# A fused mask-and-maximum pass in the second block's softmax, with the query sums put into the masks by GpSimd

## The reference

```python
def forgetting_attention(q, k, v, f, qnorm_g, knorm_g, f_bias):
    ...
    logf = jax.nn.log_sigmoid(f.astype(F32) + f_bias.astype(F32))
    c = jnp.cumsum(logf, axis=1).transpose(0, 2, 1)
    ...
        s = s + c[:, :, lo:hi, None] - c[:, :, None, :hi]
        s = jnp.where(k_pos <= q_pos, s, -jnp.inf)
        p = jax.nn.softmax(s, axis=-1).astype(dt)
```

## Time and profile before

| what | value |
|---|---|
| median of 3 runs | 1545.66 us (1545.61 to 1547.28) |
| profiled execution, its own time | 1552.2 us |
| its span, first to last instruction | 1550.3 us |
| what lies around the span | 1.9 us |
| mean granted TensorE clock | 0.993 |
| busy share of the span: PE, DVE, ACT, POOL | 98%, 77%, 66%, 5% |

### The profile page before, as it was taken

How to read it: one execution, slowest core, us unless ns; L and a number is a source line. 1 busy time by engine, 2 the same in 40 slices (tenths; PEclk the granted TensorE clock), 3 DMA queues, 4 the chain that set the end, 5 groups by cost and what they waited for, 6 DMA issues and landing times.

```text
span 1550.3 us, 27067 instructions
## 1 busy us (share of the span) xinstructions
PE 1518.6 (98%) x9990; PEld 1303.5 (84%) x9990; DVE 1186.3 (77%) x1485; ACT 1015.9 (66%) x1433; POOL 70.1 (5%) x92
## 2 busy tenths in 40 slices
PE   9999999999999999999999999999999999999998
PEld 7988888878878888899788888998788888888886
DVE  6677877775678877787776556886688888888887
ACT  6666656565566656696564445875467777777775
POOL 0000000000000000031000000120000000000000
PEclk9999999999999999999999999999899999999999
DMA  7544554544525555464154555461699999999995
GB/s 282 185 144 170 190 189 186 190 151 175 190 82 176 204 189 189 141 196 161 58 211 184 202 189 181 149 185 42 244 366 358 408 382 381 384 403 388 371 362 220
DMA packets 54795, 351.09 MB, mean 226 GB/s; under 512 B 6208, under 2 KB 9968, under 8 KB 14896
## 3 DMA queue, kind: packets, MB, share of 16 engines
q1 hardware_dynamic: 46512, 330.94, 57.2%
q0 software_dynamic: 8192, 18.90, 4.7%
HBM read 341.90 MB, written 7.91 MB: 226 GB/s over the span
## 4 chain that ended last, share of the span: by engine, by line
PE 90%; DVE 4%; ACT 3%; issue 1%; DMA 0%; POOL 0%; DVEq 0%; ACTq 0%; SPq 0%; POOLq 0%
PE PS L966 21%; PE PS L1920 16%; PE PS L2053 14%; PE PS L2089 11%; PE PS L1938 8%; PE PS L2054 8%; PE PS L1536 1%; DVE EWL L3850 1%; PE PS L2024 1%; PE PS L1901 1%; ACT MWH L2312 1%; DVE MWL L3174 1%; PE PS L1132 1%; PE PS L1038 1%; PE PS L2114 0%
## 5 line engine op out<-in xcount | busy, mean ns | idle before, releaser
L3850 DVE TENSOR_TENSOR EWL<-W,EWH 128x2048 fp32r<-128x2048 f32 x144 | 329.2, 2292 | 41.6 <-ACT EWH L2867 40.4
L2053 PE MATMUL PS<-HTB,WH 128*128 128x512 f32 x944 | 329.9, 393 | 0.0
L2867 ACT ACTIVATE EWH<-W 128x2048 fp32r<-128x2048 f32 x144 | 276.9, 1923 | 56.5 <-PE PS L1938 30.4
L2054 PE MATMUL PS<-HTB,WL 128*128 128x256 f32 x1008 | 282.5, 280 | 0.0
L3166 DVE TENSOR_TENSOR WL<-W,WH 128x2048 fp32r<-128x2048 f32 x99 | 226.5, 2288 | 35.2 <-ACT WH L2288 32.1
L2288 ACT ACTIVATE WH<-W 128x2048 fp32r<-128x2048 f32 x99 | 189.2, 1917 | 97.8 <-PE PS L2054 86.9
L966 PE MATMUL PS<-MWH,HTB 128*128 128x256 f32 (+1 forms) x940 | 240.5, 341 | 2.4 <-issue 1.5
L3174 DVE TENSOR_TENSOR MWL<-W,MWH 128x1024 fp32r<-128x1024 f32 x136 | 166.6, 1238 | 70.3 <-ACT MWH L2312 67.7
L2053 PEld LDWEIGHTS PS<-HTB,WH 128*128 128x128 f32 x944 | 177.2, 188 | 40.5
L2312 ACT ACTIVATE MWH<-W 128x1024 fp32r<-128x1024 f32 x136 | 142.3, 1055 | 83.2 <-PE PS L966 76.0
L2054 PEld LDWEIGHTS PS<-HTB,WL 128*128 128x128 f32 x1008 | 189.6, 188 | 1.0
(11 more groups left out here) (425 smaller groups left out, 2445.5 us busy)
## 6 DMA issues: line engine op xcount, KB each, us to landing
W<-in_weights SPq DMA_DIRECT2D x311, 1024.0 KB, 5.5
CS<-in_consts POOLq DMA_DIRECT2D x4, 403.5 KB, 4.8
ARENA<-rows_m POOLq DMA_DIRECT2D x8, 192.0 KB, 7.2
ARENA<-rows_m POOLq DMA_DIRECT2D x2, 768.0 KB, 12.5
moe_acc<-X POOLq DMA_DIRECT2D x3, 512.0 KB, 12.3
moe_rows<-HN POOLq DMA_DIRECT2D x3, 512.0 KB, 12.3
X<-in_x SPq DMA_DIRECT2D x2, 512.0 KB, 4.3
W<-in_weights SPq DMA_DIRECT2D x2, 512.0 KB, 6.3
```

The lines of the kernel that those rows point to most:

```text
L2053: mm(PS[b][:, :], WH[:, sl, o:o + P], HTB[:, :, kk, :], start=(kk == 0), stop=False, skip_group_check=True)
L2054: ins = mm(PS[b][:, 0:256], WL[:, sl, o:o + P], HTH[:, kk, :], start=False, stop=(kk == KC - 1), skip_group_check=True)
L2867: A(EWH[tile % SPLIT][:, :], tile_ap(w0 + tile), ACT.Copy).then_inc(sem("moe_hi"), 1)
L3850: TT(EWL[tile % SPLIT][:, :], tile_ap(w0 + tile), EWH[tile % SPLIT][:, :].bitcast(F32), SUB).then_inc(sem("moe_lo"), 1)
```

## The change

Five things:

1. DVE's `fx_softmax` does one instruction for each part of a head, `tensor_tensor_reduce`: SM = -(scores + MB), and at the same time the minimum of SM over the row, which is minus the row maximum. On DVE it is two entries in the queue, the pass itself and the reading of the accumulator. ACT takes the exponential with scale -1.
2. The bank of the scores is given free behind the fused pass, after a wait for its end.
3. The query's sum no longer enters in that pass. It is put into MB: GpSimd writes MB = causal mask + query sum, with two additions (128 x 6 x 128 and 128 x 6 x 256) in which both operands are broadcast views.
4. ACT's copy of the causal mask into MB is gone.
5. Two semaphores of each mixer are joined to one for both (names with "m2_"), with counts that go on from the first to the second.

```diff
             for r in range(2):
                 pool.dma_start(m2.KB[half[r]], rows[1, r::2].partition_broadcast(64)).then_inc(sem(m + "_kb_in"), 16)
-            pool.wait_ge(sem(m + "_gd"), 3)
+            await_free_of(pool, (m, "rowT"))
+            for t, sl in enumerate((slice(0, P), slice(P, 384))):
+                w = sl.stop - sl.start
+                pool.tensor_tensor(m2.MB[:, :, sl], bc(cst("cmask")[:, sl], 1, 6), bc(st_gc[:, t, 1, :], 2, w), ADD).then_inc(sem("masks_written"), 1)
+            pool.wait_ge(sem("masks_written"), 2 if m == "m0" else 4)
             pool.dma_start(m2.MB[:, :, 0:P], rows[2, :, 0:P].partition_broadcast(P), accum_op=ADD).then_inc(sem(m + "_mb_in"), 16)
@@ ScalarE
-                        ins = A(m2.EX[:, h % 2, sl], m2.SM[:, h % 2, sl], ACT.Exp, bias=st_mx[:, j:j + 1], accum_out=st_sum[:, j:j + 1])
+                        ins = A(m2.EX[:, h % 2, sl], m2.SM[:, h % 2, sl], ACT.Exp, scale=-1.0, bias=st_mx[:, j:j + 1], accum_out=st_sum[:, j:j + 1])
@@
             fd(13)
-            A(m2.MB, bc(cst("cmask"), 1, 6), ACT.Copy).then_inc(sem(m + "_gd"), 1)
             next_tile(5)
@@ VectorE
                 for n, sl in enumerate((slice(0, P), slice(P, 384))):
-                    ins = STT(m2.SM[:, h % 2, sl], bank(key)[:, sl], st_gc[:, n, 1, h:h + 1], m2.MB[:, h, sl], ADD, ADD)
-                release(ins, key)
-                await_free_of(dve, key)
-                for n, sl in enumerate((slice(0, P), slice(P, 384))):
-                    ins = dve.tensor_reduce(st_mx[:, 2 * h + n:2 * h + n + 1], m2.SM[:, h % 2, sl], AX.X, MAX, negate=True)
+                    ins = dve.tensor_tensor_reduce(m2.SM[:, h % 2, sl], bank(key)[:, sl], m2.MB[:, h, sl], -1.0, -NEG, ADD, MIN,
+                                                   st_mx[:, 2 * h + n:2 * h + n + 1])
                 ins.then_inc(sem(m + "f_mx"), 1)
+                dve.wait_ge(sem(m + "f_mx"), h + 1)
+                dve.sem_inc(free[uses[key][0]], 1)
```

More of the change, by code:

```diff
@@ L2660, in row_columns @@
                 rows = bank(rowT)[:, 0:48].rearrange("p (t j h) -> p t j h", t=2, j=4)
-                A(st_gc[:, :, 0, :], rows[:, :, 0, :], ACT.Copy).then_inc(sem(m + "_gc"), 1)
+                A(st_gc[:, :, 0, :], rows[:, :, 0, :], ACT.Copy).then_inc(sem("m2_gc"), 1)
                 A(st_gc[:, :, 1, :], rows[:, :, 3, :], ACT.Copy)
@@ L2694, in decays @@
                 act.wait_ge(sem(m + "_gd"), 2)
-                A(m2.DEC, m2.DEC, ACT.Exp).then_inc(sem(m + "_dec"), 1)
+                A(m2.DEC, m2.DEC, ACT.Exp).then_inc(sem("m2_dec"), 1)
                 act.wait_ge(sem(m + "_egb_in"), 32)
@@ L3530, in decayed @@
             def decayed():
-                dve.wait_ge(sem(m + "_dec"), 1)
+                dve.wait_ge(sem("m2_dec"), l + 1)
                 for r in range(2):
@@ L3629, in row_less @@
             def row_less():
-                dve.wait_ge(sem(m + "_gc"), 1)
+                dve.wait_ge(sem("m2_gc"), l + 1)
                 dve.wait_ge(sem(m + "_gd"), 1)
```

## The result

| | before | after |
|---|---|---|
| median of 7 runs each | 1546.79 us | 1550.87 us (1549.79 to 1552.50) |
| ratio, 95% interval | | 1.0028 (1.0018 to 1.0038) |
| profiled execution, its own time / span | 1552.2 / 1550.3 us | 1551.1 / 1549.3 us |

The change makes the kernel 4.1 us slower (the ratio says 0.28%). The forecast was 1551.7 us, so sign and range hold. The level is off by 0.8 us, the difference by 1.9: +6.0 was forecast, and the median of before, 1545.66 us over three runs then, is 1546.79 over seven. The three terms that make up the 4.1 us are all of another size than forecast, as the rows show.

The account below looks back on a forecast made before the run. TensorE, busy 98% of the span, was taken as the bound. Per mixer, 3.5 us of stall less 0.44 and 0.1 gave about +6 us on 1545.66, so 1551.7 us, range 1545 to 1559.

Parts of the forecast that it names:

- The stall before kk: GpSimd's additions hold up DVE's two-SBUF-input instructions, so TensorE waits 3.5 us before kk per mixer, range 2.5 to 5.
- 5.3 us in sum: GpSimd's two additions from 679.7 us: 1.8 and 3.4 us, at 2.1 ns an element plus 0.2 us each.
- Played through: Before kk, additions and DVE instructions alternate from 679.7 to 685.3 us; KB comes at 688.5 to 688.7 instead of 684.94.
- The fused pass: DVE's softmax: one pass per part instead of two saves 0.44 us per mixer at head 5, besides the banks.
- the banks: Heads 2 and 3: TensorE's wait for free score banks becomes 1.94 instead of 2.03 us, taken as -0.1 us per mixer.
- That makes 0.93 us: DVE's softmax at head 5: the pair of passes, 0.73 us, plus two accumulator readings at 0.10 us each.
- the near end, 0.73: Lowest time for head 5 on DVE, with accumulator readings costing nothing: 0.73 us, a gain of 0.64.
- ACT's copy: Removing ACT's 2.14 us mask copy at 687.04 gains 0, since ACT then waits for TensorE to free a slot.
- The clock: TensorE's clock may fall to its lower level after a stall, costing 4.3 us, at even odds per mixer.
- a sign of a wrong level: In the profile after: TensorE's clock low for longer or shorter than the 10 us after 1077.70 would show this.
- case A: Stall before kk with the clock low as often as before: 1551.7 us (1549.7 to 1554.7), chance 0.40.
- Cases C and E: Second mixer's clock fall gone: C with the stall, 1547.4 us, chance 0.08; E without it, 1540.3 us, chance 0.05.

Follow-up runs that it names:

- the copy: Against the changed kernel, GpSimd's two additions became one-input copies of the causal mask and the query's sum was left out; 1545.87 us, ratio 0.9992 to before.
- the fused pass alone: Against the changed kernel, GpSimd's additions removed, ACT copies the mask again, query's sum left out; 1544.60 us against 1546.80 before, ratio 0.9984.

## Why the prediction was right, and where it was wrong

**The stall before kk** was forecast by its mechanism: an instruction of GpSimd holds DVE's on SBUF to its end, one of 3 us too, and kk has 0.3 us of lead. The rows of after show it, and doubling, cutting up and moving the additions bear it out. The rule of the Trainium skill that the prediction weighed here (SBUF — State Buffer, two separate sides, an exclusive lock for the whole instruction) gave the right side of the two; the copy shows that here it takes no second input on GpSimd. The step that failed is the price, "5.3 us in sum". It was 4.38, a turn of DVE between the two included: 1.9 ns an element and no 0.2 us for each instruction. Played through, the additions end 5.6 us behind their start (679.7 to 685.3), so they ended 1.2 us sooner than that; DVE came 2.67 us late instead of 3.9, and TensorE waited 2.06 us before kk in place of 3.5 (the range named for it began at 2.5; the play-through's own terms, KB 3.6 to 3.8 us late less 0.3 of lead, give 3.3 to 3.5). With the 0.25 us that the half behind kk loses, the stall is 2.3 us.

**The fused pass** was forecast at -0.44 us at head 5 and -0.1 at the banks; the trace shows -0.73 at head 5 and -0.44 at the banks. The step: "That makes 0.93 us", for a head that takes 0.63. I had added 0.10 for each reading of the accumulator, and in the trace it starts together with the next pass, so that even the near end, 0.73, was too dear. From the same step come the banks: two whole heads take 1.74 us to TensorE's start (748.70 to 750.44), not 1.94 and a start, against 2.18 before. The rule of the Trainium skill (VectorE: DVE Perf Modes, rules for kernel authors), not to fuse for speed but to reduce the count, was taken in the prediction to give 0 here. The runs do not bear that out: measured are 2.2 us at an unchanged count of four: two of the four entries are no longer a pass over the data.

**ACT's copy** was forecast at nothing, and the fused pass alone, with that copy, is as fast as the sum of its waits says.

**The clock** was the large unknown and stayed one in form. It was forecast as all or nothing, a fall of 10 us that costs 4.3. What came is a fall of 3.4 us behind each stall, 1.25 us each, in the profiled execution, and in other executions of such kernels behind some stalls only. The prediction had named a sign of a wrong level, a clock low for longer or shorter than the 10 us after 1077.70, and the sign is there: those 10 us are gone in after, and two short falls stand elsewhere. Adding it up by the forecast's own terms: 2 x (3.5 - 0.54) = 5.9 against 2 x (2.3 - 1.17) = 2.3 from the mechanism, and 2 x 1.25 = 2.5 from the clock, 4.8 by the profile and 4.1 by the medians. So the total came near because an oversized stall stood in for a clock cost that case A had left out; the sign was right for the right reason, the size partly by luck.

**A premise was weak:** that before has a fall in its second mixer. The profiled execution had it, at a mean clock of 0.993. Of 72 more executions of before, beside the experiments, 66 had a mean clock of 0.995 to 0.997 (1544.7 to 1548.6 us), and six 0.993 or 0.994 (1549.3 to 1553.5 us). Cases C and E, in which that fall goes away, so had little to gain. That the profiled execution stood 6.5 us over the median was on the table and should have said as much.

## What to carry to other kernels

Before work goes to GpSimd because it is idle, look at what DVE does at that moment: beside DVE instructions with two SBUF operands it held DVE to its own end (4.38 us of additions made DVE 2.67 us late), beside those that read PSUM it was free, so the same additions cost 6.3 us in one place and nothing 27 us later. A pass that also reduces pays where TensorE waits for the softmax, and only there; the waits before TensorE's products say beforehand roughly how much (0.55 + 0.62 us of wait, 1.17 us gained). And a wait on TensorE can cost more than its own length, through the clock behind it: 1.25 us more for one of 2.1 us before kk, in some executions and not in others, and 6.2 us more for one of 1.56 us in the attention. So judge such a change on medians, and treat what one profiled execution shows of the clock as one draw.

## What the runs showed of the hardware

- GpSimd's one-input copy of 2304 elements (2.25 us) held DVE's two-SBUF-input instruction until its end, as the addition (4.38 us) did. DVE gets its turn between two instructions of GpSimd, even where they stand back to back.
- DVE's reading of the accumulator is 0.08 us and lies under the next pass; the fused pass is 0.29 us for 128 columns and 0.42 for 256, with one operand in PSUM.
- DVE copies the same 2304 elements in 1.35 us, GpSimd in 2.25.
- A wait of 2.0 to 2.1 us on TensorE between dense products was followed by 3.4 us of the lower clock in five of eight cases in the profiles, and by none in the other three; one of 1.2 us in one of two cases; waits of 3.5 and 5.6 us in all four; waits of 0.3 to 0.7 us at that place in none of four. A wait of 1.56 us between the attention's small products was followed by a stretch of 18 us at 0.54 in one of two cases.
